# Second block's state stage reordered, value products in pairs, last scatter in its own banks

## The reference

```python
for l in range(2):                      # first block
    r_q, r_k, r_v, r_g, n_q, n_kv, n_g, gm_z = split(rms_norm(x) @ w_in[l])
    mix = concat(retention(...), nsa(...), spatial_gating(...))
    x = x + mix @ w_out[l]
    x = x + (silu(gate) * up) @ w_down[l]
# second block
mod = silu(c) @ ada_w + ada_b                       # shifts, scales, gates
q, k, v, og, a_lr, u = split(modulated(x) @ w_in)
o = gla_chunked(q, k, v, log_sigmoid(a_lr @ w_alpha + b) / 16)
gla_out = rmsnorm(o, gla_norm_g) * silu(og)
y = gelu(C x_state + D u)       # x_state: complex diagonal recurrence over t
s5_out = y * sigmoid(y @ glu_w + glu_b)
h = h + g1 * rmsnorm(concat(gla_out, s5_out) @ w_out, post_g)
h = h + g2 * rmsnorm(moe(hn2), ffn_post_g)   # top 4 of 32 experts, 64-row items
```

## Time and profile before

| what | value |
|---|---|
| time, median of 3 runs | 1999.46 us (1997.54 to 2002.21) |
| time of the profiled execution | 1997.82 us |
| its span, first to last instruction | 1996.0 us |
| instructions | 22924 |
| busy: PE, PE weight load, DVE, ACT, POOL | 1887.6, 927.7, 742.0, 244.0, 225.9 us |
| mean granted TensorE clock | 0.977 |

### The profile page before, as it was taken

How to read it: one execution, slowest core, us unless ns; L and a number is a source line. 1 busy time by engine, 2 the same in 40 slices (tenths; PEclk the granted TensorE clock), 3 DMA queues, 4 the chain that set the end, 5 groups by cost and what they waited for, 6 DMA issues and landing times.

```text
span 1996.0 us, 22924 instructions
## 1 busy us (share of the span) xinstructions
PE 1887.6 (95%) x8302; PEld 927.7 (46%) x8302; DVE 742.0 (37%) x1561; ACT 244.0 (12%) x482; POOL 225.9 (11%) x401
## 2 busy tenths in 40 slices
PE   8999999999999999877799999999999999999995
PEld 4466777744667777544433333233233333333231
DVE  3553111144626871597433322222232322322233
ACT  1410000013110000121201111011011101111010
POOL 0200000002007868152000000000000000000000
PEclk9999999999999999988799999999999999999997
DMA  7143343241458854221679999999997599999993
GB/s 301 64 162 129 139 168 127 105 181 64 169 215 340 326 214 169 84 85 54 252 315 428 429 429 428 429 427 429 427 429 296 209 428 428 428 428 428 428 429 164
DMA packets 41038, 558.17 MB, mean 280 GB/s; under 512 B 4534, under 2 KB 5558, under 8 KB 6492
## 3 DMA queue, kind: packets, MB, share of 16 engines
q1 hardware_dynamic: 40508, 556.13, 67.4%
q10 hardware_dynamic: 480, 1.37, 0.2%
HBM read 556.42 MB, written 1.06 MB: 279 GB/s over the span
## 4 chain that ended last, share of the span: by engine, by line
PE 63%; DMA 23%; DVE 11%; issue 1%; ACT 1%; SPq 0%; ACTq 0%; DVEq 0%; POOLq 0%
DMA ring<-in_exp_w 22%; PE PS L1673 15%; PE PS L1954 15%; PE PS L1692 7%; PE PS L1405 7%; PE PS L1985 6%; PE PS L1577 3%; DVE ring L1106 1%; PE PS L1940 1%; PE PS L1858 1%; PE PS L1962 1%; PE PS L1460 1%; DVE tT L1324 1%; DVE tT L1321 1%; DVE tb L1325 1%
## 5 line engine op out<-in xcount | busy, mean ns | idle before, releaser
L1954 PE MATMUL PS<-ring,tb 128*64 128x512 f32 x2176 | 483.5, 597 | 23.2 <-POOLq L2084 21.3
L1954 PEld LDWEIGHTS PS<-ring,tb 128*64 128x64 f32 x2176 | 150.8, 137 | 351.3 <-issue 294.7
L1673 PE MATMUL PS<-hT,ring 128*128 128x256 f32 x1376 | 300.6, 379 | 0.0
L1673 PEld LDWEIGHTS PS<-hT,ring 128*128 128x128 f32 x1376 | 261.1, 190 | 43.0 <-issue 8.6
L1985 PE MATMUL PS<-ring,tb 128*64 128x512 f32 x1088 | 241.0, 595 | 3.7
L1405 PE MATMUL PS<-ring,hT 128*128 128x512 f32 (+2 forms) x448 | 187.3, 560 | 2.2 <-ACT hT L406 2.2
L1308 DVE TENSOR_TENSOR hT<-hT,PS 128x512 f32<-128x512 f32 x140 | 96.2, 687 | 229.4 <-PE PS L1940 222.3
L1321 DVE TENSOR_SCALAR tT<-PS 128x512 f32<-128x512 f32 x34 | 23.5, 692 | 410.2 <-PE PS L1962 410.2
L1692 PE MATMUL PS<-ring,tT 128*128 128x512 f32 x352 | 154.7, 593 | 0.0
L1985 PEld LDWEIGHTS PS<-ring,tb 128*64 128x64 f32 x1088 | 77.7, 137 | 145.1 <-issue 144.8
L1034 DVE TENSOR_TENSOR tT<-PS,tT 128x512 f32<-128x512 f32 x22 | 15.2, 692 | 269.7 <-PE PS L1673 269.7
(11 more groups left out here) (428 smaller groups left out, 1628.5 us busy)
## 6 DMA issues: line engine op xcount, KB each, us to landing
ring<-in_exp_w SPq DMA_DIRECT2D x192, 2048.0 KB, 21.2
ring<-in_w_gate_up SPq DMA_DIRECT2D x22, 2048.0 KB, 8.5
ring<-in_ada_w SPq DMA_DIRECT2D x12, 2048.0 KB, 9.3
ring<-in_w_in_part SPq DMA_DIRECT2D x10, 2048.0 KB, 10.5
ring<-in_w_down SPq DMA_DIRECT2D x10, 2048.0 KB, 7.2
ring<-in_w_out SPq DMA_DIRECT2D x6, 2048.0 KB, 8.3
ring<-in_w_in SPq DMA_DIRECT2D x4, 2048.0 KB, 7.9
ring<-in_w_in_part SPq DMA_DIRECT2D x2, 1608.0 KB, 11.8
```

What stands on the lines that cost most here:

```text
L1673: ins = pe.matmul(PS[:, 4 + 2 * (i % 2) + part, 256 * f:256 * f + 256], wt[:, k, 256 * part + 128 * f:256 * part + 128 * f + 128], hT[:, k ...
L1954: ins = pe.matmul(PS[64 * h:64 * h + 64, b, :], xg[:, o:o + 64], ring[:, s, w:w + 512], start=k == 0, stop=False, skip_group_check=True)
```

## The change

Four parts. First, the products of two heads with the values are issued together, the two of 256 columns and then the two of 128, behind the second `turn` of the pair. Second, `decayed(2)` and `decayed(3)` stand ahead of the wait for ScalarE's exponential. Third, the state stage: `states` is cut into `rotated` (four PSUM products, then the addition and subtraction, with a second temporary in `xn`), `scanned` and `rotated_back`; GpSimd keeps two of the four products of the rotation back, VectorE takes the two others one group later; the gain of the linear attention norm moves from a row product on VectorE to the scale of ScalarE's copy; GELU runs on three quarters and one, both ahead of `go_d`; TensorE's order in the stage follows (second `turn_rows` earlier, more of the input columns first). Fourth, the end: the last scatter uses banks 0, 1 and 3, 4, ScalarE squares, one VectorE product stands ahead of the root, and each half of the output is stored when it is done.

```diff
-                    if p >= 1:
-                        values(2 * p - 2)
                         turn(2 * p - 1)
...
-                        values(2 * p - 1)
+                        values(p - 1)
+                    for i, (rows, bank, o) in enumerate(at):
+                        pe.matmul(PS[rows, bank, o:o + 256], vs[i][0], PT[i][:, 0:256], start=first, stop=False, skip_group_check=True)
+                    for i, (rows, bank, o) in enumerate(at):
+                        pe.matmul(PS[rows, bank, o + 128:o + 256], vs[i][1], PT[i][:, 256:384], start=False, stop=False,
+                                  skip_group_check=True).then_inc(g.s_pv, 1)
...
                 link.to(v.tensor_tensor(pc2, pc2, st[:, 36:48].unsqueeze(2).broadcast_to([P, 12, NCMP]), ALU.subtract), g.s_c10, l + 1)
+                decayed(2)
+                decayed(3)
                 v.wait_ge(g.s_c11, l + 1)
...
+            def rotated_back(q):
+                er, ei, zi = etab[q][:, 0, :], etab[q][:, 1, :], z2[q % 2][:, 1, :]
+                v.wait_ge(g.u_pa, q + 1)
+                link(v.tensor_tensor(er, er, zi, ALU.mult))
+                link.to(v.tensor_tensor(ei, ei, zi, ALU.mult), g.u_pd, q + 1)
...
-            states(0)
-
+            rotated(0)
+            scanned(0)
+
+            rotated(1)
+            rotated_back(0)
...
-                link(pool.tensor_tensor(er, er, zi, ALU.mult))
-                link.to(pool.tensor_tensor(ei, ei, zi, ALU.mult), g.u_pd, q + 1)
+                link.to(pool.tensor_tensor(pp2[q % 2][:, 1, :], ei, zr, ALU.mult), g.u_pa, q + 1)
...
             for t in range(TT):
-                scatter_half(t, 2 * items + t + 1)
+                for h in range(2):
+                    rows = slice(64 * h, 64 * h + 64)
+                    ins = pe.matmul(PS[:, 3 * t + h, :], pwT[rows, P * t:P * t + P], ysb[rows, :], start=True, stop=True)
+                ins.then_inc(g.m_s, 1)
...
+            for t in range(TT):
+                sp.wait_ge(g.dve2, DVE2["r_done"] + t + 1)
+                sp.dma_start(out[0, P * t:P * t + P, :], x[:, t, :]).then_inc(g.s_out, 16)
```

More of the change, by code:

```diff
@@ L657, in _ @@
                 nc.scalar.activation(ysb, PS[:, 2, :], ACT.Copy).then_inc(g.m_ye, 1)
+            for t in range(TT):
+                act.wait_ge(g.m_f, t + 1)
+                nc.scalar.activation(xn[:, t, :], oacc[:, t, :], ACT.Square, accum_out=st[:, 230 + t:231 + t]).then_inc(g.m_fs, 1)
         @block.vector
@@ L1135, in _ @@
             link.to(v.scalar_tensor_tensor(lb, la, -1.0, la, ALU.mult, ALU.max), g.dve2, DVE2["al_d"] + 1)
-            states(1)
+            scanned(1)
+            rotated(2)
+            rotated_back(1)
             v.wait_ge(g.act2, ACT2["al_ln"] + 1)
@@ L1142, in _ @@
             link.to(v.tensor_tensor_scan(la[:, 256:512], K[:, K_RST:K_RST + T], lb[:, 256:512], 0.0, ALU.mult, ALU.add), g.dve2, DVE2["al_b"] + 1)
-            states(2)
+            scanned(2)
+            rotated(3)
+            rotated_back(2)
             v.wait_ge(g.act2, ACT2["al_x"] + 1)
@@ L1453, in turn, with values @@
                     ins.then_inc(g.s_tp, 1)
-                def values(c):
-                    br, h = c // NH, c % NH
-                    pe.wait_ge(g.s_pt, l * 12 + c + 1)
-                    o = (SV, WV)[br] + 64 * (h // 3)
-                    rows, bank, at = slice(64 * (h % 2), 64 * (h % 2) + 64), 6 + h // 4, 256 * (h // 2 % 2)
-                    pe.matmul(PS[rows, bank, at:at + 256], proj[:, 0, o:o + 64], PT[c % 2][:, 0:256], start=br == 0 and h in (0, 1, 4, 5), stop=False,
-                              skip_group_check=True)
-                    pe.matmul(PS[rows, bank, at + 128:at + 256], proj[:, 1, o:o + 64], PT[c % 2][:, 256:384], start=False, stop=False,
-                              skip_group_check=True).then_inc(g.s_pv, 1)
+                def values(p):
+                    pe.wait_ge(g.s_pt, l * 12 + 2 * p + 2)
+                    at, vs = [], []
+                    for c in (2 * p, 2 * p + 1):
+                        br, h = c // NH, c % NH
+                        o = (SV, WV)[br] + 64 * (h // 3)
+                        vs.append([proj[:, t, o:o + 64] for t in range(TT)])
+                        at.append((slice(64 * (h % 2), 64 * (h % 2) + 64), 6 + h // 4, 256 * (h // 2 % 2)))
+                    first = p // 3 == 0 and p % 3 in (0, 2)
+                    for i, (rows, bank, o) in enumerate(at):
[3 more added lines that the diff above has]
+                                  skip_group_check=True).then_inc(g.s_pv, 1)
                 def turn_compressed():
@@ L1740, in _ @@
             turn_rows(0, 4, g.pe2)
+            pe.wait_ge(g.dve2, DVE2["n_xn_1"] + 1)
+            turn_rows(1, 6, g.pe2)
             pe.wait_ge(g.dve2, DVE2["n_hd_0"] + 1)
@@ L1743, in _ @@
             rows(("win2", 2), 0, 4, (0, 1))
-            pe.wait_ge(g.dve2, DVE2["n_xn_1"] + 1)
-            turn_rows(1, 6, g.pe2)
-            rows(("win2", 2), 0, 4, (2, 3))
             pe.wait_ge(g.dve2, DVE2["n_hd_1"] + 1)
@@ L1753, in _ @@
             inputs(0)
+            columns(("win2", 0), 2, 7, 0).then_inc(g.u_p, 1)
+            pe.wait_ge(g.u_ea, 1)
+            columns(("win2", 0), 3, 6, 0).then_inc(g.u_p, 1)
+            inputs(1)
+            pe.wait_ge(g.u_p, 4)
+            pe.sem_inc(freed[PLACE[("win2", 0), 1][0]], 1)
             wl = p2[:, Q_WL:Q_WL + 128].rearrange("p (k n) -> p k n", k=KC)
             for k in range(KC):
-                ins = pe.matmul(PS[0:16, 7, 0:256], wl[:, k, :], hT[:, k, :], start=k == 0, stop=k == KC - 1)
+                ins = pe.matmul(PS[0:16, 5, 0:256], wl[:, k, :], hT[:, k, :], start=k == 0, stop=k == KC - 1)
             ins.then_inc(g.pe2, 1)
-            rows(("win2", 2), 0, 4, (4, 5, 6, 7)).then_inc(g.vo_p, 1)
+            rows(("win2", 2), 0, 4, (2, 3, 4, 5, 6, 7)).then_inc(g.vo_p, 1)
             pe.wait_ge(g.act2, ACT2["al_e"] + 1)
@@ L1789, in _ @@
             rows(("win2", 3), 0, 7, range(KC)).then_inc(g.vo_p, 1)
+            pe.wait_ge(g.vo_e, 2)
+            rows(("win2", 3), 1, 6, range(KC)).then_inc(g.vo_p, 1)
+            outputs(2)
             pe.wait_ge(g.dve2, DVE2["al_q"] + 1)
@@ L1802, in _ @@
             ins.then_inc(g.pe2, 1)
-            pe.wait_ge(g.vo_e, 2)
-            rows(("win2", 3), 1, 6, range(KC)).then_inc(g.vo_p, 1)
             pe.wait_ge(g.act2, ACT2["ke_e"] + 1)
@@ L1815, in _ @@
             pe.sem_inc(freed[PLACE[("win2", 3), 1][0]], 1)
-            outputs(2)
             pe.wait_ge(g.dve2, DVE2["sc_d"] + 2)
@@ L2151, in layouts @@
     column(Q_GLB, f["s5_glu_b_2"])
+    column(Q_GG, f["gla_norm_g_2"])
     q[0:16, Q_WA:Q_WA + 256] = f["w_alpha_2"][0]
```

127 lines of the change are left out of this document (57 added, 70 removed).

## The result

The changed kernel takes 1968.32 us in the median of 4 runs (1963.76 to 1970.86), the kernel before 2000.68 in the runs beside it; the ratio is 0.9839, interval 0.9823 to 0.9854. The forecast was 1968.5. The profiled execution is the fastest of the four, 1963.76 us with a span of 1962.0, so its sum is made against the 1997.82 and 1996.0 of before, and its difference (34) is not that of the medians (32).

A forecast was written before the change was run, and what follows sets the result against it. TensorE was taken to bound the first block, VectorE the state stage, TensorE and expert loads in turn the experts. Terms 8.9 + 4.4 + 8.8 + 8.0 = 30.1 off 1997.8 gave 1967.7, put at 1968.5 us; range 1958 to 1984.

The forecast's parts named there:

- Sum: Whole kernel: the four terms' gains added, 8.9 + 4.4 + 8.8 + 8.0 = 30.1 us.
- Term 1: First block, value products: two heads issued together save 0.75 us a pair, twelve pairs, taken as 8.9 us.
- rival C: First block: the two heads' values don't overlap, gain 3.6 us or less, time 1973 to 1977; chance 0.08.
- The part about alternation: Value products: two partition halves run side by side when issued alternately, as in the scores and L1954; 0.63 + 0.22 a pair.
- Term 2: First block: decayed(2) and decayed(3) earlier remove TensorE's idle, 1.4 us in layer 0, 3.0 in layer 1; 4.4.
- Term 3: State stage: VectorE's rows lengthened by GpSimd shrink, 21.9 us removed, 10.05 added, waits and half clock deducted; taken as 8.8.
- the second idle: State stage: TensorE idles about 4.9 us before outputs(3), falls to half clock, 2.3 us more.
- rival B: State stage: outputs, GLU and transposes at double cost after idles, 4 to 7 us, time 1972 to 1976; chance 0.12.
- the third idle: State stage: TensorE idles about 3.35 us before the transposes; half clock there and just after costs 2 us.
- Term 4: End of kernel: adds end 4.9 us earlier, chain behind them 2.4 shorter, last store 0.7 shorter; 8.0 in sum.
- D: State stage into mixed_2: TensorE stays at half clock, 44 us doubled, 2008 us, slower than before; chance 0.04.
- E: State stage: GpSimd's two products still delay VectorE's PSUM products or hang into SBUF work, 16 us, 1984; chance 0.11.

The follow-up runs named there:

- e12: The changed kernel run again, unaltered: 1969.39 us in the median of 4 runs.
- e11: The changed kernel plus filler products in three TensorE idles of the state stage (four, three, three): 1961.87 us in the median of 5 runs.
- e1: The changed kernel with the four value products of a pair issued head by head, not alternating: 1968.5 us (4 runs).
- e2: The changed kernel with decayed(2) and decayed(3) behind the compressed softmax again: 1972.9 us (1 run).
- e4: The kernel before, with GpSimd's four products per group cut to 8 of 1024 columns: 1980.9 us (1 run).
- e6: The changed kernel plus seven filler products on TensorE in the idle ahead of the readout alone: 1963.9 us (1 run).
- e7: The changed kernel with the second turn_rows moved back behind the first two input columns: 1970.4 us (1 run).
- e9: The changed kernel with odd heads' value products writing partitions 0 to 63, as even heads' do (results change): 1974.9 us (1 run).
- e3: The changed kernel, new order kept, with GpSimd doing all four products of the rotation back: 1974.3 us (1 run).
- e5: The changed kernel plus seven filler products in each of two TensorE idles, ahead of outputs(2) and of the readout: 1967.5 us (4 runs).
- e8: The changed kernel with the last scatter through banks 6 and 7 again and one store of the whole output: 1973.0 us (1 run).
- e10: The changed kernel plus three filler products on TensorE in the idle ahead of the readout: 1963.3 us (1 run).

## Why the prediction was right, step by step

**Sum.** 30.1 was forecast; the profile's pieces give 34.0, those of e12 29.5, the medians 32.4. The first profile's surplus is the 3.5 us in the expert piece, which no other profile shows (1029.9 to 1030.9 in twelve, the kernel before among them, and 1033.1 in e11). It lies behind the router, where the clock stayed up in that profile alone, as shown behind e11; the rhythm of the items is the same. The prediction's test, a change of more than 2 us in the experts, was therefore too strict for one profile; e12 passes it (+0.1). That 1968.5 came within 0.2 us of the median is partly luck: the errors below cancel, and the median of the kernel before moved from 1999.46 to 2000.68 between the two sets of runs.

**Term 1**, 8.9, measured 9.3 (13.7 for the first block, less 4.4). The kind of cause was right, rival C out: the products took 0.80 a pair where 0.63 + 0.22 was forecast, and the pair's period fell by the 0.75 of the sum. The part about alternation was wrong (e1). So was one of the two rows it leaned on: the scores' two products read different halves of the rows (64*128), those of the values write different halves of the columns (128*64), and L1954 alone is of their kind. By the Trainium skill's sentence on weight loads and row groups ("TensorE: Matmul & The Clock Gate", Part 3, on packing small matmuls) the pair should have gained nearly nothing, where it went from 1.60 to 0.80; the same part's 2.38 times for three column tiles is on the side of the trace.

**Term 2**, 4.4, measured 4.4 (1.4 in layer 0 and 3.0 in layer 1), with 5.9 when undone in e2. That layer 1 loses its clock was one run's accident read as a property of the layer: the term is 2.8 where no layer falls and 6.0 where both do, and 4.4 was luck as far as that goes.

**Term 3**, −8.8, measured −9.1 and −7.4, and this is where errors cancel. The removed 21.9 and the added 10.05 hold (all long rows gone; e4 gives 19.2 net of waits), the GpSimd wait was 0.97 for 1.0. But the half clock behind the second idle cost 5.8 and not 2.3: I put the idle right ahead of `outputs(3)`, while the readout stands between, and both ran at half clock, 10.4 us for 6.2 and 3.6 for 1.9. That is rival B's mechanism (a block of short products at double cost, 4 to 7 us), which I gave 0.12, short of its GLU and transposes. It also meets one of the prediction's own signs of being wrong, half clock for more than 8 us behind the new idles: it was 13.9 us behind the second alone. The other sign, expert loads that go out earlier but land no earlier, did not come. Two terms made up for it. `turn_rows` earlier, costed at nothing, gave 1.6 in the first profile and 0.3 in e12, and the third idle, costed at 2, cost 0 in the first profile, e12, e2, e6, e7 and e9, 2.5 in e1 and e3, and 1.4 to 1.7 in e5, e8 and e10. Put in, 8.8 − 3.5 + 1.6 + 2.0 = 8.9 for the 9.1 measured, so the term came out by luck.

**Term 4**, 8.0, measured 8.5: the adds 4.6 for 4.9, the chain behind them 2.5 for 2.4, and the store, the mis-sized part, 1.4 for 0.7.

**D and E** did not occur: `mixed_2` ran at full clock (27.71 us for 64) and no PSUM product beside GpSimd took over 1.23. e3 shows E's price when the beside is SBUF work.

Open is what decides whether the clock falls behind an idle of 2 to 5 us in a given run. With the idle filled the work right behind it ran at full clock in each place tried, so the idle is the cause; why the same idle brings a fall in one profile and not in another no kernel here explains.

## What to carry to other kernels

Before two engines are given equal shares of work in SBUF, read the rows of each while the other works: here one GpSimd product of 2.4 us beside VectorE's SBUF work cost VectorE 2 us and beside its PSUM work nothing, so the split follows the PSUM work's length. Price a new idle of TensorE by what stands behind it at half clock, as a chance over several profiles and not from one, and where real work can't be moved there, try a filler that ends ahead of the work that is waited for: in 3.4 us of idle, three products moved the readout by nothing and seven by 2.8 us. Products of 64 columns that write different halves of the partitions belong next to each other, in either of the two orders tried.
